# Weights multiplied into the exponentials instead of the attention outputs, and one accumulation per query row, in a hybrid attention and convolution layer

## The reference: what is computed

```python
p_c = masked_softmax(s_c, d_c >= 0)          # compressed blocks: 63 keys
o_c = einsum('bkgqn,bknd->bkgqd', p_c, v_cmp)
p_s = masked_softmax(s_s, ...)               # selected blocks
o_s = einsum('bkgqm,bkqmd->bkgqd', p_s, vs)
p_w = masked_softmax(s_w, m_w)               # window of 512 keys
o_w = einsum('bkgqm,bkmd->bkgqd', p_w, vw)
return gc[..., 0:1] * o_c + gc[..., 1:2] * o_s + gc[..., 2:3] * o_w
```

## Time and profile before

| | us |
|---|---|
| median of 3 runs | 1367.74 |
| lowest and highest | 1365.91, 1371.22 |
| span of the profiled execution, first to last instruction | 1366.2 |
| PE, DVE, ACT, POOL busy over the span | 1289.5, 935.8, 595.5, 486.1 |
| attention stage | from 289 to 592 |

### The profile page before, as it was taken

The page is one execution under the profiler, slowest core; times in us unless marked ns, Lnnn a source line. Parts: engine busy times, 40 slices in busy tenths (PEclk is TensorE's granted clock), DMA queues, the critical chain, the costliest instruction groups (busy, mean ns, idle before and its releaser), DMA issues. The chain is left out here.

```text
span 1366.2 us, 17293 instructions
## 1 busy us (share of the span) xinstructions
PE 1289.5 (94%) x6234; PEld 1051.2 (77%) x6234; DVE 935.8 (68%) x1271; ACT 595.5 (44%) x1088; POOL 486.1 (36%) x380
## 2 busy tenths in 40 slices
PE   7999999988988899989997899999999999999996
PEld 6788888866777677768886688888888887888885
DVE  6444443169887888745358888888988887655665
ACT  6211121068777877733154333333333333644541
POOL 0776400033131321110045866766676653000211
PEclk9999999999999999999999999999999999999998
DMA  5677412000000000053201232323223326965653
GB/s 224 216 266 246 155 47 93 1 20 1 1 1 1 1 1 1 1 200 124 77 32 52 109 110 91 116 93 108 85 93 116 116 87 221 351 205 178 194 179 127
DMA packets 55934, 148.24 MB, mean 109 GB/s; under 512 B 5856, under 2 KB 6368, under 8 KB 54240
## 3 DMA queue, kind: packets, MB, share of 16 engines
q1 hardware_dynamic: 47776, 111.72, 23.8%
q0 software_dynamic: 8080, 35.50, 7.2%
HBM read 107.32 MB, written 40.11 MB: 108 GB/s over the span
## 5 line engine op out<-in xcount | busy, mean ns | idle before, releaser
L497 PE MATMUL PS<-R,wh 128*128 128x512 f32 x560 | 222.5, 397 | 14.4 <-DVE wl L489 14.4
L498 PE MATMUL PS<-R,wh 128*128 128x512 f32 x560 | 219.3, 392 | 0.0
L2112 PE MATMUL PS<-R,wh 128*128 128x512 f32 x480 | 188.7, 393 | 13.2 <-DVE wl L1624 8.4
L2113 PE MATMUL PS<-R,wh 128*128 128x512 f32 x480 | 187.5, 391 | 0.0
L2114 PE MATMUL PS<-R,wl 128*128 128x512 f32 x480 | 187.4, 390 | 0.0
L501 PE MATMUL PS<-R,wl 128*128 128x512 f32 x560 | 173.3, 391 | 0.0
L497 PEld LDWEIGHTS PS<-R,wh 128*128 128x128 f32 x560 | 106.1, 189 | 38.1 <-DVE wl L489 15.2
L498 PEld LDWEIGHTS PS<-R,wh 128*128 128x128 f32 x560 | 106.2, 190 | 22.4 <-issue 0.7
L501 PEld LDWEIGHTS PS<-R,wl 128*128 128x128 f32 x560 | 105.7, 189 | 22.3
L2126 PE MATMUL PS<-R,wh 128*128 128x512 f32 x308 | 120.6, 392 | 0.4 <-DVE R L1714 0.2
L2128 PE MATMUL PS<-R,wl 128*128 128x512 f32 x308 | 119.9, 389 | 0.0
(11 more groups left out here) (232 smaller groups left out, 2685.0 us busy)
## 6 DMA issues: line engine op xcount, KB each, us to landing
raw<-in_w_units SPq DMA_DIRECT2D x55, 512.0 KB, 3.6
F<-gated SPq DMA_DIRECT2D x77, 256.0 KB, 4.0
W<-in_w_units POOLq DMA_DIRECT2D x11, 1024.0 KB, 7.8
weight_sums<-W POOLq DMA_DIRECT2D x11, 1024.0 KB, 4.9
raw<-weight_sums SPq DMA_DIRECT2D x44, 256.0 KB, 4.0
F<-in_w_units SPq DMA_DIRECT2D x20, 512.0 KB, 4.5
gated<-F SPq DMA_DIRECT2D x33, 256.0 KB, 2.1
raw<-in_w_units SPq DMA_DIRECT2D x33, 256.0 KB, 3.3
```

What stands on the lines that cost most here:

```text
L497: nc.tensor.matmul(out, w_h, hi(kt)[:, cols], start=first, stop=False)
L498: nc.tensor.matmul(out, w_h, lo(kt)[:, cols], start=False, stop=False)
L2112: nc.tensor.matmul(out, w_h, operand(name, k, 0), start=fresh and k == 0, stop=False, skip_group_check=not fresh)
L2113: nc.tensor.matmul(out, w_h, operand(name, k, 1), start=False, stop=False, skip_group_check=not fresh)
```

## The change

The weight, gate over denominator, is multiplied into the exponentials before they are turned. So all branches of a row can be summed in one PSUM accumulation, and the group becomes the row: 16 instead of 48.

- POOL multiplies the compressed part of all four heads and the other parts of heads 0 to 2 in place (`weigh(n)`), ACT those of head 3 (`weigh_head`, in unit 4n+6). PE's `turn_step` waits for both.
- Steps run two blocks behind the scores instead of one (`BLOCK_LAG = 2`), so three blocks of exponentials live at once: `E` becomes one area of 10,240 columns with places from a table, and `E_C` a ring of three.
- `copy_out`, `turn_out`, `add_halves` run once per row, and DVE writes the row directly to its place; POOL's products and sums of the outputs are gone.

```diff
-STEPS, GROUPS, BLOCK_AT = [], [], []
+STEPS, BLOCK_AT = [], []
...
-LAST_OF = {last: group for group, (_, _, _, last) in enumerate(GROUPS)}
+LAST_OF = {last: row for row, last in enumerate(ROW_LAST)}
...
+BLOCK_LAG = 2
+NU_END = NU + BLOCK_LAG * GROUP
 def steps_behind(unit):
-    n, h = divmod(unit, GROUP)
-    if n == 0:
+    n, h = divmod(unit - BLOCK_LAG * GROUP, GROUP)
+    if n < 0:
         return range(0)
-    first, count = BLOCK_AT[n - 1], BLOCK_AT[n] - BLOCK_AT[n - 1]
+    first, count = BLOCK_AT[n], BLOCK_AT[n + 1] - BLOCK_AT[n]
...
-        E = [[F1[:, 11 + h, :] for h in range(GROUP)], [F1[:, 5 + h, :] for h in range(GROUP)]]
+        E = F1[:, 5:15, :].rearrange("p a b -> p (a b)")
+        E_C = PBm[:, 0:3 * GROUP * CW].rearrange("p (r h n) -> p r h n", r=3, h=GROUP)
...
+            def weigh(n):
+                _, i, _ = BLOCKS[n]
                 pool.wait_ge(coef_ready, n + 1)
+                weights = lambda br, h, count=1: factor[:, i % 4, br * GROUP + h:br * GROUP + h + count]
+                if has_compressed(n):
+                    e = E_C[:, ROWS[n] % 3, :, :]
+                    nc.gpsimd.tensor_tensor(e, e, weights(CMP, 0, GROUP).rearrange("p (h o) -> p h o", o=1)
+                                            .broadcast_to([P, GROUP, CW]), ALU.mult)
+                for h in range(GROUP - 1):
+                    for br, _, count, e in unit_parts(GROUP * n + h):
+                        if br != CMP:
+                            last = nc.gpsimd.tensor_tensor(e, e, weights(br, h).broadcast_to([P, count]), ALU.mult)
+                last.then_inc(es_ready, 1)
...
+                if U % GROUP == 0 and 0 < U <= NU:
+                    weigh(U // GROUP - 1)
...
             def head_squares(row):
-                act.wait_ge(o_ready, row + 1)
+                act.wait_ge(t_used, O_OF[row] + 1)
...
+            def weigh_head(n, h):
+                _, i, _ = BLOCKS[n]
+                act.wait_ge(coef_ready, n + 1)
+                for br, _, _, e in unit_parts(GROUP * n + h):
+                    if br != CMP:
+                        last = nc.scalar.activation(e, e, ACT.Copy, scale=factor[:, i % 4, br * GROUP + h:br * GROUP + h + 1])
+                last.then_inc(eh_ready, 1)
...
+                if U % GROUP == 2 and GROUP < U <= NU + 2:
+                    weigh_head(U // GROUP - 1, GROUP - 1)
...
-                nc.vector.tensor_reduce(OS[:, i % 2, br, :].rearrange("p (h d) -> p h d", d=DH),
-                                        PS[:, T_BANK + at % T_RING, :].rearrange("p (h e d) -> p h d e", e=2, d=DH), AX.X, ALU.add)\
+                nc.vector.tensor_reduce(F1[:, Q0 + 2 * g:Q0 + 2 * g + 2, i * P:(i + 1) * P].rearrange("p a (b d) -> p a b d", d=DH),
+                                        PS[:, T_BANK + at % T_RING, :].rearrange("p (a b e d) -> p a b d e", a=2, b=2, e=2),
...
             def turn_step(s):
-                pe.wait_ge(ex_ready, GROUP * (n + 1))
+                pe.wait_ge(es_ready, n + 1)
+                pe.wait_ge(eh_ready, n + 1)
...
             def values(s):
-                _, _, first, end = GROUPS[group]
+                first, end = ROW_FIRST[row], ROW_LAST[row]
```

More of the change, by code:

```diff
@@ L141, in unit_at @@
     return GROUP * ROWS.index(TT * g + i)
[L144 removed]
+STEPS, BLOCK_AT = [], []
 for n_block, (g_block, i_block, kind_block) in enumerate(BLOCKS):
     BLOCK_AT.append(len(STEPS))
[L147 to L149 removed]
+    STEPS += [(n_block, br_block, j_tile) for br_block, tiles in branches(i_block, kind_block) for j_tile in tiles]
 BLOCK_AT.append(len(STEPS))
[L151 removed]
+NS, NROWS = len(STEPS), KV * TT
+ROW_STEPS = [[s for s, (n_block, _, _) in enumerate(STEPS) if ROWS[n_block] == row] for row in range(NROWS)]
+ROW_FIRST, ROW_LAST = [at[0] for at in ROW_STEPS], [at[-1] for at in ROW_STEPS]
 PV_LAG, COPY_LAG, TURN_LAG, SQUARE_LAG = 2, 2, 4, 8
@@ L897, in _ @@
+            for U in range(NU_END):
                 if U in QUERIES_AT and QUERIES_AT[U][2] % 2 == 0:
                     queries(*QUERIES_AT[U])
-                for s in steps_behind(U):
-                    behind(s)
-            for s in range(NS, END):
-                behind(s)
+                if U % GROUP == 0 and 0 < U <= NU:
+                    weigh(U // GROUP - 1)
             pool.wait_ge(osq_ready, KV * TT)
@@ L1151, in behind @@
                     later_values_hi(s)
-                group = LAST_OF.get(s - SQUARE_LAG)
-                if group in ROW_OF:
-                    head_squares(ROW_OF[group])
+                if s - SQUARE_LAG in LAST_OF:
+                    head_squares(LAST_OF[s - SQUARE_LAG])
+            def weigh_head(n, h):
[5 more added lines that the diff above has]
+                last.then_inc(eh_ready, 1)
             waiting = None
-            for U in range(NU + GROUP):
+            for U in range(NU_END):
                 if U in QUERIES_AT and QUERIES_AT[U][2] % 2:
@@ L1980, in values @@
             def values(s):
-                n, br, j, group = STEPS[s]
-                g, _, _ = BLOCKS[n]
-                _, _, first, end = GROUPS[group]
+                n, br, j = STEPS[s]
+                g, row = BLOCKS[n][0], ROWS[n]
+                first, end = ROW_FIRST[row], ROW_LAST[row]
                 pe.wait_ge(t_used, T_OF[s] + 1)
-                if s == first and group:
-                    pe.wait_ge(ot_copied, group)
+                if s == first and row:
+                    pe.wait_ge(ot_copied, row)
                 elif s == first:
                     pe.wait_ge(vc_lo, KV)
-                if s == first and ROWS[n] == TT:
+                if s == first and row == TT:
                     pe.wait_ge(t_used, V_OF[VALUES_AT[-1]] + 1)
```

99 lines of the change are left out of this document (43 added, 56 removed).

## The result

The changed kernel takes 1379.15 us (median of 4 runs, 1378.69 to 1381.31), the kernel before, in the same measurement, 1368.45 (4 runs, 1365.91 to 1371.22): a ratio of 1.0085, 95% interval [1.0068, 1.0102]. It is slower by 11.6 us, where 14.5 us less were forecast. The profiled execution's span is 1377.6 us (before 1366.2), its mean granted clock 0.974 (before 0.985).

What follows compares the result with a forecast made beforehand. It took PE's own work to bound the attention stage late and the exponentials early. Gains of 30 us against 1 + 13 + 1.5 added gave -14.5 us, hence 1353.2 us, with 1339 to 1374 holding 8 of 10.

Steps and rivals of the forecast that it cites:

- turns: On PE, 32 of the 48 turns of the output go, at 0.43 us each: 13 us gained.
- bank waits: PE's waits for the output bank's copy: 47 group boundaries become 15, 7 us gained.
- relief: 32 copies leave ACT and 32 reductions DVE: 2 us gained early, where these engines pace the scores.
- tail: End of the stage: POOL and one of two reductions leave the chain before the squares, 3 us gained.
- two blocks behind: Later steps: 5 us gained on waits for a block's own exponentials, 1.5 us lost at the emptier start.
- the deadline: POOL must finish a block's multiplications before PE turns it; shortfalls in some blocks cost PE 13 us, the largest added term.
- ACT's head: ACT's 32 multiplications, 20.7 us busy, about what the copies give back; 1 us on the path (0 to 5).
- The prediction's own mark of error: Wrong if a 1024-column multiplication takes over 2.6 us, or PE's wait for exponentials grows by what the turns gave back.
- The second: Rival: PE's savings return as waits for the exponentials; half of the 30 us remain, time 1367.7 us; chance 0.18.
- The first: Rival: POOL is the bound, at 2.86 ns a column; 1370.4 us, more with clock drops; chance 0.20.
- the third: Rival: the deadlines don't bind because real units are longer; 13 becomes 3, time 1343.2 us; chance 0.19.
- The fourth: Rival: POOL's multiplications lock DVE out of key and query preparation, +5.5 us, time 1358.7 us; chance 0.10.

Runs made afterwards that it cites:

- no_weights_lag1: Changed kernel without any multiplication of the exponentials and with steps one block behind as before: 1352.26 us, ratio 0.9888 to the kernel before.
- no_weights: Changed kernel with the multiplications on POOL and ACT left out, PE waiting for the exponentials alone: 1358.11 us, ratio 0.9926 to the kernel before.
- after: The changed kernel itself, with all parts of the change: 1379.15 us, ratio 1.0085 to the kernel before.
- act_twice: Changed kernel with each of ACT's 32 multiplications done twice, once into a place nobody reads: 1393.45 us, ratio 1.0193 to the kernel before.
- experiment 1: Changed kernel without weights, with the lag (1358.11 us) and without (1352.26 us); its table splits several kernels' time into units 0 to 103 and the tail.
- lag2_only: Kernel before with its steps two blocks behind and the exponentials' places much as in the change: 1374.37 us, ratio 1.0054.
- experiment 6: ACT's multiplications moved, or three unused PE products added ahead of units 4 to 8: 1370.59 us with queries prepared earlier, 1356.20 us without weights.
- experiment 4: Changed kernel with POOL's query preparation up to four units earlier in its queue, ahead of the multiplications: 1373.97 us, ratio 1.0049 to the kernel before.
- head_on_vector: Changed kernel with head 3 multiplied on DVE behind the factors instead of on ACT: 1386.70 us, ratio 1.0139 to the kernel before.
- all_edits: Changed kernel with alternating block order, earlier POOL query preparation, ACT's multiplications ahead of the exponentials and additional PE products at the start: 1368.39 us, ratio 1.0005.
- experiments 4 and 5: Changed kernel with POOL's query preparation earlier (1373.97 us), or with light and heavy blocks alternating in order (1370.37 us); both edits together took 1371.14 us.
- alternate: Changed kernel with light and heavy blocks in the other order every second row: 1370.37 us, ratio 1.0023 to the kernel before.

## Why the prediction was wrong

Its account and the measured one, against the kernel before:

| part | forecast | measured | by |
|---|---|---|---|
| one accumulation (turns, bank waits, relief, tail) | -25 | -15.3 | no_weights_lag1 |
| two blocks behind (start +1.5, own exponentials -5) | -3.5 | +5.2 | no_weights over no_weights_lag1 |
| weights (POOL +13, ACT +1) | +14 | +21.7 | after over no_weights |
| sum | -14.5 | +11.6 | |

**The failed step is how the waits were booked.** Waits of PE that go were taken as time won at their full length: 7 us for the bank, 2 of relief, 5 for a block's own exponentials. Of the waits that come, only the deadline (13) and 1 us for ACT's head had a price, the later steps 1.5, and a lower clock none. The sum holds only if PE doesn't wait elsewhere instead and keeps its speed. In `no_weights_lag1` PE's busy time up to the last product fell by 12.8 us, as the 13 for the turns had it, but its waiting went from 30.6 to 32.1 us, where 9 were to go: the copy's 4.2 us less came back with 6.9 us more of waits for exponentials. With the lag and the weights its waiting rose by another 13.4 us, and its same 1596 instructions took 11.4 us longer at the lower clock. The range "leaves out the clock drops"; they came.

Two readings of the prediction are to be kept apart here. "Late in the stage PE's own work is the price of everything" holds for the turns: in the second KV head (units 52 to 103) `no_weights_lag1` takes 128.7 us for 135.0, and the 16 turns gone there are 6.9 us by their price. But a PE that is busy 29.8 of 30 us doesn't show that the other engines have room: in after, work added to ACT costs 0.6 of its length (`act_twice`). The scores wait for a pair of banks, the banks for the exponentials on ACT, these for the maximum on DVE, and the steps' high and low parts stand in the same two queues.

The prediction's own mark of error came in part: at the scores PE waits 10 us more for the exponentials (8.9 to 19.1 at the matmuls, 17.1 to 26.5 at the weight loads), where the turns were to give 13. Of its other signs, POOL's wait is 6 to 7 us for 10 to 15, the copy's 9.2 for at most 4, the stage to the first of the last squares 312 us for 288, DVE's fall 12 for 20.

**Turns 13, bank waits 7, relief 2, tail 3.** The counts were right, the sum ten too large. How the 15.3 us split was not tried one by one. The table of experiment 1 puts 10.2 us of them into the units, 1.0 into the tail, and the weight split behind it gave 2.5 as forecast. Bank waits went from 10.8 to 6.6 us in `no_weights_lag1` and to 9.2 in after, not by 7: fewer copies, but each can stand on ACT behind an exponential of 1024 columns. One of the two longest, in the timeline of after:
```profile
422.30 0.64 PE L2021 MATMUL PS<-R 63*128 63x512 f32 x1 [2.70 <-ACT F L1154]
```

**Two blocks behind: the sign was wrong.** "The 14 steps instead of 6 behind the last scores cost no extra PE time" is the sentence. The steps behind the last scores were booked only at the start, where they were missing, at 1.5 us; behind the units they cost 6.5, and 7.5 in `lag2_only`, without any of the other edits. The units should have become shorter for it and did not; in the profiles the low clock of the start accounts for some 3 us of that, and by the times of experiment 6 keeping PE at work gives 1 to 4 us. The 5 us for the blocks' own exponentials never reached the end: in `no_weights` the turns wait 0.2 us for them, but the scores 16.7 us and the products 9.4 for the copy (11.0 and 6.6 with the lag of one). They were also read too large. The earlier trace rows adds the waits of weight loads and matmuls, which are the same seven stalls: 4.2 us at the matmuls and not 9.8.

**ACT's head: +1 forecast, 6.4 to 13.4 measured.** Its price in busy time was nearly right (23.0 us against 20.7). Wrong was to set off "about what the copies give back" and then count only the one instruction that stands ahead of an exponential. The copies' relief is already in the 15.3 us of one accumulation and can't pay for the head a second time.

**POOL's heads: +13 forecast, 8.3 to 15.3 measured, for another reason.** The multiplication took 1.895 us at 1024 columns, under the 2.16 taken, far from the 2.6 named as the limit; POOL's busy time came out at 130.6 for 140. PE's wait for it is 6 to 7 us and not 13, so the deadline binds half as hard. But "its inputs are old, so it runs in POOL's idle time" failed: the inputs were old, the queue was not free, and the consumer was DVE, which stands in the pacing loop. Moving the preparation gave 4.9 us (experiment 4). The deadline was seen for PE and not for DVE's wait on the same queue.

**The rivals.** The second, that what PE saves comes back as waits for the exponentials, had half of the mechanism with 1367.7 us, 11 too low: the waits came back, the turns' own work did not, and it too left the lag at its start's price. The first, POOL as the bound, had the sign but is refuted in its cause: the price per column is below the forecast's, not above. The clock drops that it added came without it: the mean clock up to the last product is 0.93 for 0.98. Of the third half came true. The fourth came in part: in after, the 12 preparations of L1489 took 849 ns in the mean for 686, and the ten of L1476 and L1495 with two tiles of SBUF 2.5 us more in all than in `no_weights_lag1`, together 4.5 us of its 11; the instructions from PSUM stayed at 687 ns (L1564).

**DVE beside POOL.** In `head_on_vector` DVE's tensor_scalar with one input in SBUF took 1153 ns in the mean for 512 columns, where the same kind took 480 to 486 ns in the kernel before (L1579, 8 of them, with POOL idle beside them). This is the Trainium skill's rule ("SBUF — State Buffer", "Who interferes with whom"), that a DVE instruction in a 2-port mode holds GpSimd and is held by it like one with two SBUF inputs; the trace agrees, if this instruction is in such a mode, which no row shows. In `all_edits` it shows from the other side: POOL's 256 columns, 0.61 us in the earlier trace rows, took 1.53 us beside an instruction of DVE that reads two tiles.
```profile
577.28 1.22 DVE L522 TENSOR_TENSOR wl<-raw,wh 128x1024 fp32r<-128x1024 f32 x1
...
577.44 1.53 POOL L910 TENSOR_TENSOR PBm<-PBm,factor 128x256 f32<-128x256 f32 x1 [6.13 <-DVE factor L1552]
```

**Still open.** How much of the 11.4 us that PE's same instructions take longer would be won at a full clock: only the low clock of the stage's start was lifted, for 3.8 and 1.2 us. Why experiments 4 and 5 don't add up; how ACT's 6.4 to 13.4 us divide between its amount and POOL's overlap; and how much of after's loss is the pairing of heavy with heavy blocks by itself, since `alternate` changes POOL's deadlines as well. No version with the weights in the exponentials beat the kernel before. The fastest kernel run, `no_weights_lag1`, leaves the weights out: its 15.3 us are what this design with one block of lag gives if the weights cost nothing.

## What to carry to other kernels

An engine busy 99% doesn't show that the others have room: lengthen another one's work by a known amount, as in `act_twice`, and see what part of it reaches the end. A wait that goes is a gain only if no other one grows: compare the sum of the waits, not one line of them, and count a stall once where weight load and matmul both show it. Compare also the busy time of the same instructions, in which a lower clock shows. Steps moved behind a loop cost their length there, and the loop need not get shorter. When long instructions enter an in-order queue, list everything behind them and each one's consumer, not only the consumer of the new work.

## What the runs showed of the hardware

- POOL's product with a factor held constant over the columns is cheaper per column than its sum of two tiles: 1.895 us for 1024 columns and 1.255 for 640, against 1.364 for 512.
- A multiplication by a factor per partition on ACT, SBUF to SBUF, takes 1.146 us for 1024 columns and 0.828 for 640.
- With 12 us of scores alone, PE 9.99 us busy at the low rate, the granted clock stood at 0.50; three products more per unit in five units held it at 1.00.
- The same 1596 instructions of PE were busy 250.9 us at a mean granted clock of 0.97, 257.4 at 0.94 and 262.2 at 0.93 (`no_weights_lag1`, `no_weights`, after).
- A DVE tensor_scalar of 640 columns, SBUF to SBUF, started 0.04 to 0.05 us ahead of a POOL multiplication took 0.55 us once, with POOL's 640 columns at 1.62 us, and 1.65 us another time, with POOL's at 1.25.
